# A float32r transformer block on one core: weight tiles interleaved in three of five buffer pairs, one pair's moving columns read by halves, and the buffers 256 bytes further on

## The reference

```
x = first_block(x, c, ctx, ...)        # proj = h @ w_in; branches; (...) @ w_o; relu(h @ w1)**2 @ w2
return second_block(x, meta_tokens_2, ...)  # h @ attn_w_in; attention; @ attn_w_out; pool mixer
```

## Time and profile before

| what | value |
|---|---|
| time before, median of 2 runs | 2738.11 us (2733.66 to 2742.55) |
| the profiled execution | 2743.35 us |
| its span, first to last instruction | 2741.5 us |
| TensorE busy | 2687.8 us (98%) |
| VectorE busy | 1906.2 us (70%) |
| ScalarE busy | 1268.6 us (46%) |
| TensorE clock granted, mean of the span | 0.992 |
| DMA moved | 539.01 MB, 197 GB/s in the mean |

### The profile page before, as it was taken

One profiled execution on the slowest core, in us unless ns is written; L12 is line 12 of the kernel. 1 busy time (PEld: TensorE's weight loads), 2 busy tenths in 40 slices (PEclk: granted clock), 3 DMA queues, 4 the chain that ended last, 5 costly groups with the idle time before them and its releaser, 6 DMA issues.

```text
span 2741.5 us, 51493 instructions
## 1 busy us (share of the span) xinstructions
PE 2687.8 (98%) x21464; PEld 2567.7 (94%) x21464; DVE 1906.2 (70%) x2933; ACT 1268.6 (46%) x1836; POOL 154.7 (6%) x162
## 2 busy tenths in 40 slices
PE   7999999999999999999999999999999999999998
PEld 4599977899999999999999999999999999989997
DVE  6765689889897778886554655677656665478564
ACT  5522344455446444544443444464444444544453
POOL 0000011200014001100000000030000000100001
PEclk9999999999999999999999999999999999999999
DMA  8766765466666788787556555564444444536564
GB/s 307 287 219 218 240 190 177 135 201 186 198 185 195 253 281 266 260 284 230 185 185 197 180 192 186 186 198 154 157 136 146 157 148 150 173 120 189 186 196 130
DMA packets 163990, 539.01 MB, mean 197 GB/s; under 512 B 31024, under 2 KB 35120, under 8 KB 163632
## 3 DMA queue, kind: packets, MB, share of 16 engines
q1 hardware_dynamic: 163760, 535.73, 59.8%
HBM read 533.57 MB, written 2.10 MB: 195 GB/s over the span
## 4 chain that ended last, share of the span: by engine, by line
PE 91%; DVE 5%; DMA 1%; issue 1%; ACT 1%; SPq 0%; POOL 0%; DVEq 0%; ACTq 0%
PE ps L566 27%; PE ps L571 27%; PE ps L568 27%; DVE lo L1690 1%; PE ps L782 1%; PE ps L801 1%; PE ps L729 1%; DMA raw<-in_w_mod 1%; PE ps L717 1%; PE ps L790 1%; DVE row L2265 1%; PE ps L957 0%; PE ps L745 0%; DMA raw<-in_w_in 0%; PE ps L979 0%
## 5 line engine op out<-in xcount | busy, mean ns | idle before, releaser
L1076 ACT ACTIVATE hi<-raw 128x1024 fp32r<-128x1024 f32 x856 | 900.9, 1057 | 914.1 <-PE ps L571 471.1
L566 PE MATMUL ps<-AH,hi 128*128 128x256 f32 (+2 forms) x4432 | 1263.2, 285 | 1.8 <-DVE AL L2104 1.8
L571 PE MATMUL ps<-AH,lo 128*128 128x256 f32 (+2 forms) x4432 | 1251.8, 282 | 7.5 <-DVE lo L1690 7.4
L568 PE MATMUL ps<-AL,hi 128*128 128x256 f32 (+2 forms) x4432 | 1252.9, 283 | 0.0
L1690 DVE TENSOR_TENSOR lo<-raw,hi 128x1024 fp32r<-128x1024 f32 x856 | 1038.8, 1227 | 201.8 <-ACT hi L1076 200.1
L566 PEld LDWEIGHTS ps<-AH,hi 128*128 128x128 f32 x4432 | 836.7, 189 | 31.1 <-issue 28.3
L571 PEld LDWEIGHTS ps<-AH,lo 128*128 128x128 f32 x4432 | 837.1, 189 | 10.8 <-DVE lo L1690 10.7
L568 PEld LDWEIGHTS ps<-AL,hi 128*128 128x128 f32 x4432 | 836.4, 189 | 0.9
L566 PE MATMUL ps<-YH,hi 128*128 128x256 f32 (+1 forms) x1512 | 422.6, 279 | 0.0
L568 PE MATMUL ps<-YL,hi 128*128 128x256 f32 (+1 forms) x1512 | 422.6, 279 | 0.0
L571 PE MATMUL ps<-YH,lo 128*128 128x256 f32 (+1 forms) x1512 | 422.4, 279 | 0.1
(11 more groups left out here) (276 smaller groups left out, 2510.0 us busy)
## 6 DMA issues: line engine op xcount, KB each, us to landing
raw<-in_w_ff SPq DMA_DIRECT2D x256, 512.0 KB, 4.3
raw<-in_w_in SPq DMA_DIRECT2D x208, 512.0 KB, 4.2
raw<-in_w_mod SPq DMA_DIRECT2D x192, 512.0 KB, 4.9
raw<-in_w_ain SPq DMA_DIRECT2D x128, 512.0 KB, 3.7
raw<-in_w_pin SPq DMA_DIRECT2D x64, 512.0 KB, 3.5
raw<-in_w_o SPq DMA_DIRECT2D x32, 512.0 KB, 4.7
raw<-in_w_aout SPq DMA_DIRECT2D x32, 512.0 KB, 3.6
raw<-in_w_pout SPq DMA_DIRECT2D x32, 512.0 KB, 3.5
```

Of the source, the lines that this page charges most:

```text
L566: e.matmul(b.ap[:, o], hi[:, k, :], xh, start=start and k + i == 0, stop=False, skip_group_check=many)
L568: e.matmul(b.ap[:, o], hi[:, k, :], xl, start=False, stop=False, skip_group_check=many)
L571: mm = e.matmul(b.ap[:, o], los[j % NSPLIT][:, k, :], xh, start=False, stop=stop and k == KU - 1, skip_group_check=many)
L1076: e.activation(his[u % NSPLIT][:, :, :], raws[raw_at[i]][:, :].rearrange("p (k m) -> p k m", k=KU), ACT.Copy).then_inc(s_hi, 1)
```

## The change

Four things change together. Nothing is computed otherwise: the same products are summed, in the same order over k.

1. `pad` grows from 16 to 80 floats and `after` shrinks from 128 to 64: the raw and split buffers lie 256 bytes further on (320 bytes behind the activations modulo 1024), and all that follows them stays where it was.
2. In pairs 1, 2 and 3 (from split unit 52 on) the tiles are interleaved by 2, 4 and 8: column m of tile k stands at float (k // g) * 128 g + m g + k % g. TensorE then loads 128 weights with a step of 8, 16 or 32 bytes. Pairs 0 and 4 stay as they were (g = 1, step of 4 bytes).
3. ScalarE and VectorE read the raw unit in one run as before, and write (VectorE also reads `hi`) with that step.
4. In pair 4, where the moving side has exactly 256 columns and the code is `unit`'s, columns 0 to 15 are followed by 128 to 143, then 16 to 31, 144 to 159 and so on: runs of 16 floats (64 bytes), from the first and the second half in turn. The output is written to PSUM in the same order of places, so each result lands where it did.

```
+GROUPS = (1, 2, 4, 8, 1)
+TURNED = (False, False, False, False, True)
+def spread(t, u, k=None):
+    g = GROUPS[u % NSPLIT] if u >= FIRST else 1
+    w = t[:, :, :].rearrange("p k m -> p (k m)").rearrange("p (a m b) -> p a b m", b=g, m=128)
+    return w if k is None else w[:, k // g, k % g, :]
+def inorder(t, u):
+    g = GROUPS[u % NSPLIT] if u >= FIRST else 1
+    return t[:, :].rearrange("p (a b m) -> p a b m", b=g, m=128)
+def banks(x, turned):
+    return x.rearrange("p (h l c) -> p l h c", h=2, c=16) if turned else x
...
-        pad = sb("pad", [128, 16])
+        pad = sb("pad", [128, 80])
...
-        sb("after", [128, 128])
+        sb("after", [128, 64])
...
-                        e.matmul(b.ap[:, o], hi[:, k, :], xh, start=start and k + i == 0, stop=False,
+                        turned = xh.shape[1] == T and TURNED[j % NSPLIT]
+                        y, xh, xl = banks(b.ap[:, o], turned), banks(xh, turned), banks(xl, turned)
+                        e.matmul(y, spread(hi, j, k), xh, start=start and k + i == 0, stop=False,
...
-                e.activation(his[u % NSPLIT][:, :, :], raws[raw_at[i]][:, :].rearrange("p (k m) -> p k m", k=KU),
-                             ACT.Copy).then_inc(s_hi, 1)
+                e.activation(spread(his[u % NSPLIT], u), inorder(raws[raw_at[i]], u), ACT.Copy).then_inc(s_hi, 1)
...
-                e.tensor_tensor(los[u % NSPLIT][:, :, :], raws[raw_at[i]][:, :].rearrange("p (k m) -> p k m", k=KU),
-                                his[u % NSPLIT][:, :, :].bitcast(F32), ALU.subtract).then_inc(s_lo, 1)
+                e.tensor_tensor(spread(los[u % NSPLIT], u), inorder(raws[raw_at[i]], u),
+                                spread(his[u % NSPLIT], u).bitcast(F32), ALU.subtract).then_inc(s_lo, 1)
```

More of the change, by code:

```diff
@@ L565, in unit @@
                     for i, (xh, xl, o) in enumerate(parts(k0 + k)):
-                        e.matmul(b.ap[:, o], hi[:, k, :], xh, start=start and k + i == 0, stop=False,
+                        turned = xh.shape[1] == T and TURNED[j % NSPLIT]
+                        y, xh, xl = banks(b.ap[:, o], turned), banks(xh, turned), banks(xl, turned)
+                        e.matmul(y, spread(hi, j, k), xh, start=start and k + i == 0, stop=False,
                                  skip_group_check=many)
-                        e.matmul(b.ap[:, o], hi[:, k, :], xl, start=False, stop=False, skip_group_check=many)
+                        e.matmul(y, spread(hi, j, k), xl, start=False, stop=False, skip_group_check=many)
                         if k + i == 0:
                             e.wait_ge(s_lo, j + 1)
-                        mm = e.matmul(b.ap[:, o], los[j % NSPLIT][:, k, :], xh, start=False,
+                        mm = e.matmul(y, spread(lo, j, k), xh, start=False,
                                       stop=stop and k == KU - 1, skip_group_check=many)
@@ L596, in units_together @@
                             e.wait_ge(s_hi, j0 + i + 1)
-                        e.matmul(b.ap[:, o], hi[:, k, :], xh, start=start and k == 0, stop=False)
-                        e.matmul(b.ap[:, o], hi[:, k, :], xl, start=False, stop=False)
+                        e.matmul(b.ap[:, o], spread(hi, j0 + i, k), xh, start=start and k == 0, stop=False)
+                        e.matmul(b.ap[:, o], spread(hi, j0 + i, k), xl, start=False, stop=False)
                         if k == 0:
                             e.wait_ge(s_lo, j0 + i + 1)
-                        mm = e.matmul(b.ap[:, o], lo[:, k, :], xh, start=False, stop=stop and k == KU - 1)
+                        mm = e.matmul(b.ap[:, o], spread(lo, j0 + i, k), xh, start=False, stop=stop and k == KU - 1)
                         if k == KU - 1:
@@ L1047, in _ @@
                                 e.wait_ge(s_al, 48 + kt + 1)
-                            e.matmul(b.ap[:, 0:T], hi[:, 4 * mi + k, :], Y1H[:, kt, :], start=(k == 0), stop=False)
-                            e.matmul(b.ap[:, 0:T], hi[:, 4 * mi + k, :], Y1L[:, kt, :], start=False, stop=False)
+                            e.matmul(b.ap[:, 0:T], spread(hi, j, 4 * mi + k), Y1H[:, kt, :], start=(k == 0), stop=False)
+                            e.matmul(b.ap[:, 0:T], spread(hi, j, 4 * mi + k), Y1L[:, kt, :], start=False, stop=False)
                             if mi == k == 0:
                                 e.wait_ge(s_lo, j + 1)
-                            mm = e.matmul(b.ap[:, 0:T], lo[:, 4 * mi + k, :], Y1H[:, kt, :], start=False, stop=(k == 3))
+                            mm = e.matmul(b.ap[:, 0:T], spread(lo, j, 4 * mi + k), Y1H[:, kt, :], start=False, stop=(k == 3))
                         mm.then_inc(s_unit if mi else s_grp, 1)
```

## The result

The changed kernel takes 3717.08 us (3717.01 to 3717.15), the kernel before 2738.11: a ratio of 1.3575 (1.3481 to 1.367), 979 us more. The forecast was 3505 us with a range up to 3640: the likeliest case came, and the change cost 28% more than the 767 us forecast for it. Ratios compare fast executions alone; of e1's ten, one at 3764 us (granted clock 0.65) and one at 5905 us (granted clock 1.00) are left out, and nothing here shows why the second took so long.

The account below looks back on a forecast made before the run. TensorE, busy 98%, was taken as the bound, with weight loads and matmuls level. Stepped loads in pairs 2 and 3 add 767 us, all else 0: 2743.35 to 3510, less 5 for the median, 3505 us; range 2690 to 3640, likeliest alone 3300 to 3640.

Parts of the forecast that it names:

- the likeliest case: Whole kernel: TensorE's loads with steps of 16 and 32 bytes cost +767 us, giving 3505 us; chance 0.46.
- 128 x 1.63 = 209 ns, and with the 5 ns or so around it, it comes every 214 ns: TensorE's weight loads in pairs 2 and 3: priced from VectorE's L2166, +96 ns on 7,988 matmuls, +767 us.
- The upper end: Stepped weight loads in pairs 2 and 3: at most 223 ns, twice 105 ns plus 13 ns, +839 us.
- a dense matmul (113 ns) is already as short as its weight load lets it be: TensorE's dense matmuls: loads and matmuls are level, so a slower load shows in full.
- rival B: Pairs 1 to 3: meetings of load and moving read go away, down to 112 ns; 2665 us, chance 0.06.
- the 16-byte line as the unit of the price: TensorE's weight loads: steps of 4 and 8 bytes are free, steps of 16 and 32 are not.
- the reason given: Shift by 256 bytes: taken at 0, since the stretch at 2545 us visits that place too; +20 to -12 us.
- pair 1 and pair 4 were taken at 0: Pair 1's 8-byte step and pair 4's halves: 0 each; ends +383 to -24 us and +278 to -7 us.
- up to +30 us: Slower splitting on VectorE: what it adds if a step is free on TensorE, cover being thin at 1040 us.
- A: Pairs 2 and 3: the step is free for TensorE; 2748 us, 2695 to 2790, chance 0.24.
- C: Pairs 2 and 3: more meetings of load and moving read, 25 ns a matmul, +200, 2938 us; chance 0.14.
- D: Pair 4: the broken PSUM write costs while the step is free, up to +278, 3016 us; chance 0.10.

Follow-up runs that it names:

- e1: Changed kernel with only the shift by 256 bytes left, no tile interleaved and no columns by halves; ratio 0.9994 to the kernel before.
- e13: Changed kernel with pairs 2 and 3 left at a step of 4 bytes; 2763.97 us, ratio 1.0085 to the kernel before.
- e7: Kernel before, with weight loads of 96, 64 or 32 columns in three of five output tiles; 2727 us against 2745 beside it, one execution.
- e8: Kernel before, 256 moving columns cut to 64 or 128, weights read at steps of 1, 4, 8, 5 floats; stepped loads 233, 239, 222 ns at half clock.
- e4: Changed kernel, writers dense, no halves, TensorE alone reading weights at steps of 3, 5, 6, 7 and 0 floats in pairs 0 to 4; 4271 us.
- e9: Kernel before with the split buffers 128 bytes behind the activations in place of 64, nothing interleaved; 2785.71 us, ratio 1.0141.
- e5: Changed kernel, nothing interleaved, 256 moving columns read by halves in runs of 4, 8, 32, 16 floats in pairs 1 to 4, output written straight on; 2806 us.
- e3: Changed kernel without halves, ScalarE and VectorE using the steps but TensorE loading dense runs; 2810.88 us, ratio 1.0239 to the kernel before.
- e6: Changed kernel, nothing interleaved, moving columns read straight on, PSUM output written by halves in runs of 4, 8, 32, 16 floats in pairs 1 to 4; 2741 us.

## Why the prediction was right in kind and short in size

**The account.** Pair 2: 235 - 118 = 117 ns on 3,994 matmuls, 467 us. Pair 3: 242 - 118 = 124 ns, 495 us. Pairs 1 and 4: 26 us (e13). The shift: 0 (e1). Together 988 us, measured 979. The step of 16 and 32 bytes on TensorE's loads is 962 of it.

**The term that was mis-sized** is "128 x 1.63 = 209 ns, and with the 5 ns or so around it, it comes every 214 ns". It measured 235 ns at 16 bytes and 242 at 32, +117 and +124 in place of +96: 195 us of the 212 by which the forecast fell short. The 1.63 ns came from L2166, a single VectorE reduction with a step of 64 bytes. VectorE's own splitting now shows a larger price: L1708 rises from 1.22 us to 2.08 at 16 bytes and 2.24 at 32 (means by pair), which is 1.87 and 2.04 ns a float once the 0.16 us of fixed cost are taken off (1.04 without a step), and TensorE's 1.83 and 1.88 are near these. So the kind of reading was right, a price for each line touched, and the row was a poor scale. That the price is one and the same whoever asks is not shown: the splitting has two stepped operands, L2166 has one, and the figures run from 1.63 to 2.04 ns. Why a step of 64 bytes gave less on VectorE was not tried.

**The upper end** (223 ns) was wrong as a bound. It took a stepped load for at most double one that streams without a step, which nothing in the trace said. With 250 ns as that end the range would have held the result; it missed by 77 us.

**A step that failed without harm:** "a dense matmul (113 ns) is already as short as its weight load lets it be". e7 refutes it. The moving side takes 113.3 ns by itself, and the load, 112 ns when it is alone (e8), lies just under it. Two numbers close to each other were taken for cause and effect. The conclusion survived, since a load of 235 ns overtakes either; but rival B's floor of 112 ns was then out of reach too, and no layout of the weights could be expected to bring the dense stages below 113: loads of a quarter of the columns did not (e7), nor did a step of 0 (e4).

**Right:** the 16-byte line as the unit of the price (pair 1 at 121 ns, not 235; e4 shows it); the shift (e1: 0), though by luck: the reason given, that the place is one which the stretch at 2545 us visits, holds for a shift to 128 bytes too, and that costs 40 us (e9); the count of matmuls; that no wait takes part and that the slow splitting is covered in this kernel. **Wrong by little:** pair 1 and pair 4 were taken at 0 and cost 26 us. For pair 4 the read was taken as free from VectorE's L2162; on TensorE it costs 5 ns (e5). Its count of 2,458 has the 192 matmuls of the groups in it, which are not read by halves; that makes under 1 us. **Wrong where it did not count:** uncovered, the slow writes cost 67 us (e3) where "up to +30 us" stood. VectorE's price was larger there too (1.87 to 2.04 ns a float), and time was short in more stages than the one named; how the 67 us divide between the two was not tried.

**The rivals.** A and B: pairs 2 and 3 would have stayed near 118. C, more meetings: it stood at 130 to 160 ns, and e8 shows 233 ns with a quarter of the moving read. D, the broken PSUM output: e6, nothing.

**Lines of 16 and of 8 bytes.** The Trainium skill (Advanced Engine Details and Errata, section SBUF Cachelines) asks for two hits on a 16-byte line. These runs agree and put numbers to it for weight loads: four hits 118 ns in the mean of all shapes, two 121 (256 columns), one and a third 174, one 227 to 242. Its section PSUM Cachelines says any non-contiguous pattern slows matmuls significantly, and that every two consecutive elements should lie together. Here outputs in runs of 16 bytes and more, which keep pairs together, cost nothing (e6, 115 to 117 ns); the measurement decides for such runs, and shorter ones were not tried.

## What to carry to other kernels

Before an operand gets a step, count the 16-byte lines that it touches: on this chip a float32r weight load costs about 1.8 ns a line once that is more than the 113 ns of a 256-column matmul, so a step of 8 bytes is nearly free (121 ns), 12 bytes takes 174 and 16 bytes doubles the matmul. Here a price taken from one row of another engine gave the sign and the border, and was a fifth too small (767 us for 962); the upper end of a range that rests on such a row has to lie well above it. Two durations that agree within a few ns are no proof that one sets the other: narrow one of them and look.

## What was not expected of the hardware

A float32r matmul of 256 columns takes 113.3 ns at 2.4 GHz, not 107, even with weight loads of 32 columns (e7). In the kernel before most units hold 113.3 or some 118 ns from end to end (225 and 141 of the 475 units with 256 columns). The place of the weights relative to the moving tiles matters: 64 and 320 bytes behind cost the same (e1), 128 bytes 1.4% more in total (e9); other places were not tried. Reading the moving side in turns from two places 512 bytes apart costs 4 to 11 ns a matmul of 256 columns, with runs of 32 down to 4 floats (e5). And a load with a step of 16 bytes takes 233 ns at either clock, while one without a step goes from 112 to 214 ns when the clock falls to 0.50 (e8).
